# Moving the end of an expert chunk into the next chunk, and reading the expert weights in rows of 2 KB instead of 16 KB

## The reference, cut to what matters

```python
def expert_ffn(xb, wg, wu, wd):
    return (jax.nn.silu(xb @ wg) * (xb @ wu)) @ wd
...
    h2 = rms_norm(x, lp['norm2_g'])
    moe = hier_moe(h2.reshape(B * T, D), ...)      # sum over a token's two experts of gate * expert_ffn(h2)
    x = x + moe.reshape(B, T, D)
...
    y_prompt = rms_norm(yp, final_norm_g)          # and the same for y_sample
```

## Time and profile before

| | |
|---|---|
| time, median of 3 runs | 1856.1 us (1854.3 to 1857.44) |
| the profiled execution's own time | 1861.37 us |
| its span, first to last instruction | 1859.8 us |
| the first half and the router, up to the first chunk's matmuls | 868.6 us |
| 32 chunks, from there to the start of the last one | 944.0 us |
| the last chunk and what comes behind it | 47.2 us |

### The profile page before, as it was taken

How to read it: one execution, slowest core, us unless ns; L and a number is a source line. 1 busy time by engine, 2 the same in 40 slices (tenths; PEclk the granted TensorE clock), 3 DMA queues, 4 the chain that set the end, 5 groups by cost and what they waited for, 6 DMA issues and landing times.

```text
span 1859.8 us, 29119 instructions
## 1 busy us (share of the span) xinstructions
PE 1715.0 (92%) x10574; PEld 1464.1 (79%) x10574; DVE 704.1 (38%) x1890; ACT 371.7 (20%) x799; POOL 491.3 (26%) x872
## 2 busy tenths in 40 slices
PE   7999999999999999975999999999898789698985
PEld 4767676767676767655999999998898789688985
DVE  3446464636363636453232222222223132222232
ACT  2313131313131313121121111110101011101111
POOL 1001010101111111112333333333434243334444
PEclk9999999999999999995999999999999899799997
DMA  9310101010202020255887988888888788767761
GB/s 310 121 69 24 68 23 68 23 68 7 83 0 90 0 79 1 58 142 188 266 298 256 318 300 277 289 281 298 277 297 283 258 278 291 280 239 285 259 207 51
DMA packets 89329, 325.76 MB, mean 175 GB/s; under 512 B 31653, under 2 KB 32582, under 8 KB 81094
## 3 DMA queue, kind: packets, MB, share of 16 engines
q1 hardware_dynamic: 56870, 253.67, 38.5%
q0 software_dynamic: 32416, 71.49, 12.5%
HBM read 283.66 MB, written 65.98 MB: 188 GB/s over the span
## 4 chain that ended last, share of the span: by engine, by line
PE 54%; DMA 23%; issue 9%; POOL 6%; DVE 5%; POOLq 2%; ACT 1%; DVEq 1%; ACTq 0%; SPq 0%
PE ps L703 18%; DMA gate_sb<-acc_rows,idx_out 14%; PE ps L764 13%; PE ps L726 6%; DMA acc_rows<-w_out_sb,idx_out 6%; PE ps L839 6%; PE ps L851 3%; DVE w_out_sb L1326 3%; DMA idx_in<-slot_table 2%; PE ps L785 2%; PE ps L736 1%; POOL acc_rows L655 1%; DVE gate_sb L1333 1%; POOL out_y L671 1%; POOL pad L339 1%
## 5 line engine op out<-in xcount | busy, mean ns | idle before, releaser
L839 PE MATMUL ps<-w_out_sb,w_in_sb 128*128 128x156 f32 (+4 forms) x3072 | 395.8, 286 | 1.3 <-ACT w_out_sb L978 1.3
L839 PEld LDWEIGHTS ps<-w_out_sb,w_in_sb 128*128 128x128 f32 x3072 | 387.5, 190 | 1.6 <-issue 1.6
L339 POOL TENSOR_TENSOR pad<-mhalf 128x1 f32<-128x1 f32 x260 | 57.2, 220 | 1169.3 <-DMA idx_in<-slot_table 272.6
L703 PE MATMUL ps<-cols_sb,w_in_sb 128*128 128x256 f32 (+1 forms) x1728 | 360.5, 369 | 2.7 <-issue 2.7
L703 PEld LDWEIGHTS ps<-cols_sb,w_in_sb 128*128 128x128 f32 x1728 | 313.6, 191 | 45.9 <-issue 6.9
L764 PE MATMUL ps<-w_out_sb,cols_sb 128*128 128x512 f32 x544 | 236.7, 596 | 5.5 <-DVE cols_sb L1156 5.5
L764 PEld LDWEIGHTS ps<-w_out_sb,cols_sb 128*128 128x128 f32 x544 | 103.3, 191 | 132.6 <-issue 126.7
L991 ACT ACTIVATE w_out_sb<-w_out_sb 78x1024 f32<-78x1024 f32 (+4 forms) x64 | 67.6, 1057 | 605.6 <-DVE w_out_sb L1326 604.6
L851 PE MATMUL ps<-w_out_sb,cols_sb 128*128 128x156 f32 (+4 forms) x1024 | 151.5, 317 | 22.2 <-DVE w_out_sb L1316 22.2
L851 PEld LDWEIGHTS ps<-w_out_sb,cols_sb 128*128 128x128 f32 x1024 | 148.5, 218 | 23.6 <-DVE w_out_sb L1316 23.6
L1326 DVE SCALAR_TENSOR_TENSOR w_out_sb<-ps,idx_out,gate_sb 64x512 f32<-64x512 f32 (+4 forms) x128 | 87.0, 738 | 205.8 <-DMA gate_sb<-acc_rows,idx_out 205.8
(11 more groups left out here) (194 smaller groups left out, 1593.0 us busy)
## 6 DMA issues: line engine op xcount, KB each, us to landing
w_in_sb<-in_w_gate SPq DMA_DIRECT2D x32, 2048.0 KB, 8.9
w_in_sb<-in_w_up SPq DMA_DIRECT2D x16, 2048.0 KB, 16.2
w_in_sb<-in_w_down SPq DMA_DIRECT2D x16, 2048.0 KB, 13.5
rows_sb<-in_w_up SPq DMA_DIRECT2D x16, 2048.0 KB, 15.8
cols_sb<-in_w_down SPq DMA_DIRECT2D x16, 2048.0 KB, 12.2
rows_sb<-in_x SPq DMA_DIRECT2D x34, 512.0 KB, 3.7
acc_rows<-rows_sb SPq DMA_DIRECT2D x17, 512.0 KB, 2.6
h_rows<-cols_sb SPq DMA_DIRECT2D x17, 512.0 KB, 2.7
```

Of the source, the lines that this page charges most:

```text
L339: return eng.tensor_tensor(pad[:, n:n + 1], mhalf[:, 0:1], mhalf[:, 0:1], ALU.mult)
L703: mm = pe.matmul(bank[:, cc * n:(cc + 1) * n], w_in_v[:, k, col:col + P], hT[:, k, 0:n], start=(k == 0), stop=(k == KD - 1))
L839: mm = pe.matmul(bank[:, m * CH:m * CH + size], w[:, k, f * P:(f + 1) * P], xTm[:, k, :, 0:size // 2], start=(k == 0), stop=(k == KD - 1))
```

## The change

The parts, of which the sixth concerns the first half:

1. The `r` banks are evicted plainly: ACT copies `r00` and `r10`, DVE `r01` and `r11`, each 512 columns, into `ysb`.
2. Gate and addition become two instructions of DVE from SBUF (`add_rows`), which run in the next chunk, behind its first L1316. The sums of squares (`row_squares`) stand on ACT behind the next chunk's second Silu, the scaling (`norm_rows`) on DVE behind its third L1316.
3. POOL's loop starts with the scatter of the chunk before and its root, waits for that scatter to land, gathers `part` for its own chunk, scatters the finished rows of the chunk before, and then loads `idx_in` and gathers `xg`. Ahead of the loop there is a gather of `part` with a list that names no row, and behind it the root and the output of the last chunk.
4. Gate and up matrices are read as eight rows of 2 KB per partition. (The down matrix was read in rows of 4 KB before and still is.)
5. New semaphores order this: `added`, `none_loaded`.
6. `h2` is written in its natural order, by the same instruction without the strided view, and the router's two small matrices are loaded row by row to match.

```diff
 def gate_up(e, i):
     for dst, src in ((wg_e[i], a["w_gate"]), (wu_e[i], a["w_up"])):
-        sp.dma_start(dst.rearrange("p k f -> p (k f)"), src.rearrange("e (p k) f -> e p (k f)", p=P)[bass.ds(e, 1)]
-                     .rearrange("a p n -> p (a n)")).then_inc(w_loaded[i][0], 16)
+        sp.dma_start(dst, src.rearrange("e (k p) f -> e p k f", p=P)[bass.ds(e, 1)]
+                     .rearrange("a p k f -> p (a k) f")).then_inc(w_loaded[i][0], 16)
...
+load_index_at(NE * SLOTS, idx_out, none_loaded)
...
+def roots(n):
+    pool.wait_ge(y_stored, 32 * n + 32)
+    pool.wait_ge(ysq_ready, 2 * n + 3)
+    carried(6 * n + 2)
+    nc.gpsimd.tensor_copy(idx_y[:], idx_out[:]).then_inc(iy_ready, 1)
...
+pool.wait_ge(none_loaded, 16)
+fetch_rows()
+with pool.Fori(0, chunks) as q:
+    pool.wait_ge(added, 2 * q + 2)
+    carried(6 * q + 1)
...
+    roots(q)
+    pool.wait_ge(nx_loaded, 16 * q + 16)
+    pool.wait_ge(iy_ready, q + 1)
+    pool.wait_ge(part_stored, 32 * q + 32)
+    carried(6 * q + 3)
+    nc.gpsimd.tensor_copy(idx_out[:], idx_nx[:]).then_inc(io_ready, 1)
+    pool.wait_ge(io_ready, q + 1)
+    carried(6 * q + 4)
+    fetch_rows()
+    load_index(q + 1, idx_nx, nx_loaded)
+    store_rows(q, 6 * q + 5)
...
+def row_squares(n):                                  # ACT
+    for h in range(2):
+        act.wait_ge(added, 2 * n + 1 + h)
+        act.wait_ge(ysq_ready, 2 * n + 1 + h)
+        act.wait_ge(yrs_ready, n + 1)
+        nc.scalar.activation(junk, ysb[:, h], ACT.Square, accum_out=ssq[0:HF, h:h + 1]).then_inc(ysq_ready, 1)
...
+    act.wait_ge(part_stored, 32 * q + 32)
+    act.wait_ge(yfin_ready, 2 * q + 2)
+    for i in range(2):
+        bank = wait_full(act, "chunk", q, f"r{i}0")
+        nc.scalar.copy(ysb[0:size // 2, 0, i * BANK:(i + 1) * BANK], bank[0:size // 2, :])\
+            .then_inc(read("chunk", f"r{i}0"), 1)
...
+def add_rows(n):                                     # DVE
+    dve.wait_ge(part_loaded, 32 * n + 32)
+    for h in range(2):
...
+        V.scalar_tensor_tensor(out=ysb[:, h], in0=ysb[:, h], scalar=idx_out[:, h, 1:2].bitcast(F32),
+                               in1=part[:, h], op0=ALU.mult, op1=ALU.add).then_inc(added, 1)
+
+def norm_rows(n):
+    dve.wait_ge(yrs_ready, n + 2)
...
-    V.scalar_tensor_tensor(out=by_k(h2[:, t], 0), in0=by_k(xr[:, t], 1), scalar=rstd[:, GT + t:GT + t + 1],
-                           in1=by_k(g2b[:], 1), op0=ALU.mult, op1=ALU.mult).then_inc(h2_ready[t], 1)
+    V.scalar_tensor_tensor(out=h2[:, t], in0=xr[:, t], scalar=rstd[:, GT + t:GT + t + 1], in1=g2b[:],
+                           op0=ALU.mult, op1=ALU.mult).then_inc(h2_ready[t], 1)
```

More of the change, by code:

```diff
@@ L297, in hymba_step @@
         nx_loaded = sem("nx_loaded")
+        none_loaded = sem("none_loaded")
         io_ready = sem("io_ready")
@@ L300, in hymba_step @@
         part_stored = sem("part_stored")
+        added = sem("added")
         iy_ready = sem("iy_ready")
@@ L390, in _ @@
                 (rb[:], a["router_b"].broadcast_to([P, NG + NE])),
[L391 to L392 removed]
+                (rw[:, :, 0:NG], a["router_gw"].rearrange("(k p) n -> p k n", p=P)),
+                (rw[:, :, NG:NG + NE], a["router_ew"].rearrange("(k p) n -> p k n", p=P)),
             ]
@@ L627, in _, with fetch_rows @@
                 pool.dma_start(idx_y[:, h, :], table[0:CH].rearrange("(p h) c -> p h c", h=2)[:, h, :]).then_inc(y_stored, 16)
+            load_index_at(NE * SLOTS, idx_out, none_loaded)
             pool.nop().then_inc(yrs_ready, 1)
             pool.nop().then_inc(moe_carry, 1)
[L630 to L636, removed]
+            def fetch_rows():
                 for h in range(2):
@@ L646, in _ @@
                 wait_full(pool, "chunk", q, "xT3")
-                carried(5 * q + 3)
+                carried(6 * q + 6)
                 gather()
[L650 to L674, removed]
+            carried(6 * chunks + 1)
+            roots(chunks)
+            pool.wait_ge(iy_ready, chunks + 1)
+            store_rows(chunks, 6 * chunks + 3)
             pool.wait_ge(xg_loaded, 32 * chunks + 64)
             pool.wait_ge(nx_loaded, 16 * chunks + 16)
-            pool.wait_ge(y_stored, 32 * chunks + 32)
+            pool.wait_ge(part_stored, 32 * chunks)
+            pool.wait_ge(y_stored, 32 * chunks + 64)
         @block.tensor
@@ L979, in x_columns @@
                         .then_inc(read(seg, f"xT{j}"), 1)
+            def row_squares(n):
+                for h in range(2):
+                    act.wait_ge(added, 2 * n + 1 + h)
+                    act.wait_ge(ysq_ready, 2 * n + 1 + h)
+                    act.wait_ge(yrs_ready, n + 1)
+                    nc.scalar.activation(junk, ysb[:, h], ACT.Square, accum_out=ssq[0:HF, h:h + 1]).then_inc(ysq_ready, 1)
             def chunk(q, size):
@@ L984, in chunk @@
                     nc.scalar.activation(sg[:, f, 0:size], bank[:, 0:size], ACT.Silu).then_inc(sg_ready, 1)
+                    if f == 1:
+                        row_squares(q)
                 x_columns("chunk", q, size)
[L986 to L992, removed]
+                act.wait_ge(part_stored, 32 * q + 32)
[4 more added lines that the diff above has]
+                        .then_inc(read("chunk", f"r{i}0"), 1)
             act.nop().then_inc(ysq_ready, 1)
@@ L1000, in _ @@
                     chunk(q, size)
+            row_squares(ends[-1])
         @block.vector
@@ L1310, in _ @@
             ends = size_ends(dve)
+            def add_rows(n):
+                dve.wait_ge(part_loaded, 32 * n + 32)
+                for h in range(2):
+                    for i in range(2):
+                        wait(dve, read("chunk", f"r{i}{h}"), JOBS.before("chunk", n, f"xT{2 * i + h}"))
+                    V.scalar_tensor_tensor(out=ysb[:, h], in0=ysb[:, h], scalar=idx_out[:, h, 1:2].bitcast(F32),
+                                           in1=part[:, h], op0=ALU.mult, op1=ALU.add).then_inc(added, 1)
+            def norm_rows(n):
+                dve.wait_ge(yrs_ready, n + 2)
+                dve.wait_ge(y_stored, 32 * n + 32)
+                for h in range(2):
+                    V.scalar_tensor_tensor(out=yfin[:, h], in0=ysb[:, h], scalar=rstd[0:HF, h:h + 1],
+                                           in1=g1b[0:HF], op0=ALU.mult, op1=ALU.mult).then_inc(yfin_ready, 1)
             def chunk(q, size):
@@ L1317, in chunk @@
                         .then_inc(read("chunk", f"gu{f}"), 1)
+                    if f == 0:
+                        add_rows(q)
+                    if f == 2:
+                        norm_rows(q)
                 for j in PAIRS:
@@ L1320, in chunk @@
                     V.tensor_copy(yT[:, 2 * j:2 * j + 2, 0:size], pair(bank, size)).then_inc(read("chunk", f"y{j}"), 1)
-                dve.wait_ge(io_ready, q + 1)
-                dve.wait_ge(part_loaded, 32 * q + 32)
+                dve.wait_ge(part_stored, 32 * q + 32)
+                dve.wait_ge(ysq_ready, 2 * q + 3)
                 for i in range(2):
[L1324 to L1334, removed]
+                    bank = wait_full(dve, "chunk", q, f"r{i}1")
+                    V.tensor_copy(ysb[0:size // 2, 1, i * BANK:(i + 1) * BANK], bank[0:size // 2, :])\
+                        .then_inc(read("chunk", f"r{i}1"), 1)
             dve.wait_ge(fg_loaded, 16)
@@ L1339, in _ @@
                     chunk(q, size)
+            add_rows(ends[-1])
+            norm_rows(ends[-1])
 def kernel(**inputs):
```

15 lines of the change are left out of this document (13 added, 2 removed).

## The result

The changed kernel takes 1803.25 us (median of 4 runs, 1799.3 to 1806.86), the kernel before 1856.77 beside it (1854.3 to 1863.93): a ratio of 0.9705, 95% interval 0.9669 to 0.9741. The forecast was 1804. As the experiments show, that figure hides two effects of opposite sign: the rows of 2 KB alone give more than the whole gain, and the new order takes some 18 us of it back. Two executions (one of the kernel before, one of `pieces_4kb_b`) took far longer than every other of the same kernel, 3,710 and 8,421 us, and are left out of the times and ratios measured here (the 1820 in a later expectation still has the second in it).

The account below looks back on a forecast made before the run. POOL's round was taken to bound the last 19 periods. Short periods 54.5, chunks of 156 4.4 and `h2` 0.8 less, start 8 more: 51.7 us off 1861.4, 1809.7, or 1804 on the runs' scale; forecast 1780 to 1835, whole range 1755 to 1875.

Parts of the forecast that it names:

- POOL's round sets the pace of the short chunks: Last 19 periods, 30.37 us each: POOL's round, not PE, sets them; changed round forecast at 27.5 us.
- The 1.2 us: POOL's round in the kernel before: its terms summed to 29.2 us, within 1.2 of the mean period; half was kept.
- landing with root: POOL's round: root leaves the path, the scatter's whole landing takes its place, 6.1 us a round.
- The short periods: The 19 periods of the last three stretches: from 30.37 to 27.5 us each, 54.5 us less.
- the chunks of 156: Chunks of 156 slots: a round falls below PE's own work, stretch from 234.7 to 230.3 us, 4.4 less.
- The first chunk: Ahead of the loop: empty list and gather, then added steps, delay PE's down matmuls to 900, 8 us once.
- The 0.8 us of `h2`: L1170 without the strided view: 0.8 us shorter 17 times, but counted only behind the last tile, 0.8 us.
- The 2 KB pieces decide: POOL's queue beside gate and up loads: 82 GB/s instead of 51, so 3 us less waiting for `idx_in` a round.
- Without any help from the queue a round is 29.8 us: POOL's round, pieces giving nothing: 14.0 + 6.1 + 9.7 us; as a rival about 1875 us, chance 0.07.
- the slower rival: POOL's wait for `part_stored` ahead of the gather: long landings, pieces no help, round 32.6, 1932 us; chance 0.16.
- PE alone: Short stretches: POOL's round falls below PE's work, 470 us instead of 577, 1752 us in all; chance 0.10.
- The DMA engines as bound: Short periods: DMA work with some idle time leaves 28.5 us, 1823 in all; chance 0.09 with other smaller gains.

Follow-up runs that it names:

- pieces_4kb_b: The changed kernel with gate and up read in 4 KB pieces, two neighbouring rows each, `h2` paired to match: 1813.65 us, ratio 0.9751 to the kernel before.
- rows_only: The kernel before with the 2 KB rows and the matching order of `h2` and router matrices, old eviction and order: 1785.19 us, ratio 0.9614.
- order_only: The changed kernel with gate and up in 16 KB pieces and strided `h2` as before, new round kept: 1952.01 us, ratio 1.0486 to the kernel before.
- start_early: The changed kernel with the empty list loaded at POOL's first lists and its gather issued early: 1794.54 us, ratio 0.9633 to the kernel before.
- rows_strided: The kernel before with only gate and up read as 2 KB rows, `h2` still strided: 1788.78 us, ratio 0.9624.
- rows_list: The kernel before with the 2 KB rows and `idx_in`'s load at the head of POOL's round: 1785.21 us, ratio 0.9576.
- list_start: The changed kernel with `idx_in`'s load ahead of the gather of `part`, and the empty list and its gather early: 1774.75 us, ratio 0.9523 to the kernel before.

## Why the prediction was right, and where it was not

**POOL's round sets the pace of the short chunks: right.** The round's parts, with POOL's waits of the 19 short rounds alone: 14.0 of issuing, 1.4 of root and 4.1 (77.3/19) of landing, 7.4 (141.2/19) of list, 26.9 us; the 19 periods are 27.2 each, forecast 27.5. The 1.2 us that the forecast's sum for the kernel before left open came of waits averaged over the whole second half: in its 19 short rounds the list is 188.3/19 = 9.9 and the scatter 42.4/19 = 2.2, and 14.0 + 4.1 + 9.9 + 2.2 = 30.2 of 30.4. Two terms were off and cancelled, which was luck: landing with root is 5.5 where the forecast had 6.1, the list 7.4 where it had 6.7. The rest of the distance to 27.5 is half of that 1.2.

**Term by term.** The short periods gave 60.7 us (forecast 54.5) and the chunks of 156 gave 7.5 (4.4), because the chunks of 156 had the higher level of the clock, 2.4 GHz, throughout (1.00). The first chunk cost 8.4 (8): POOL waited for the empty list, the gather went out at 884.53, and PE began its down matmuls 6.0 us late:

```profile
884.53 1.07 POOL L636 DMA_INDIRECT gate_sb<-acc_rows,idx_out  x1 [8.39 <-DMA idx_out<-slot_table]
...
898.48 12.03 PE L870 MATMUL ps<-w_out_sb,w_in_sb 128*128 128x180 f32 x64 [7.39 <-DVE w_out_sb L1355]
```

The forecast had 900 for that start, 1.5 more; what makes the 8 come out is that the matmuls themselves then took 12.03 us, where they took 9.96 before, at a mean granted clock of 0.84 instead of 1.00. The forecast had no such term. DVE's extra work, 1.1 us a chunk by the forecast, is 1.4 in the chunks of 132 (54.86 against 46.44 over six), and lies beside other work. The 0.8 us of `h2` can't be told from nothing.

**The 2 KB pieces decide: right, and shown; where they act, only in part.** The step took 82 GB/s for POOL's queue beside them; the stretch above shows 128. In the old order the pieces do what the forecast said: the list falls from 9.9 to 7.2 us a short round (137.7/19 in `rows_only`). In the new order the list hardly falls, from 8.2 in `order_only` (155.7/19) to 7.4, and the landing with root falls from 12.1 (1.4 + 204.0/19) to 5.5. The forecast kept the landing at 6.1 with or without the pieces. Why the list fell by less than the rate of the queue rose is not shown. The Trainium skill (DMA: Bandwidth & Descriptors, "Queues, rings and completion order") gives a typical packet, the unit in which an engine changes queues, as some 9 to 17 descriptors; read as widely as a whole load's share it would have given nothing, and the pieces gave 72 us. Whether the number itself holds here the counts above do not show. The same page's section "SWDGE vs HWDGE vs iDMA" calls a packet that GpSimd writes preferably at most 4096 bytes; the rows of POOL's queue here are 4096 bytes each, and the page says no such thing of SP's pieces.

**"Without any help from the queue a round is 29.8 us: one wait replaces another, and nothing is won": wrong.** `order_only` is that case, and its 19 periods are 34.0 us. The term that failed is the landing. I took 6.1 us from the old order, where most rounds never waited; in the short rounds of the new one it is the 12.1 above. The round becomes 14.0 + 12.1 + 8.2 = 34.3. That is the slower rival, which I had at 32.6 and 1932 us and to which I gave 0.16: its place was right and its price near, its condition (no help from the pieces) did not hold for the changed kernel, and the load that its scatter meets is gate and up, not the down matrix. I had not seen that a late round of POOL puts the scatter beside that load in most short rounds.

**So the total was right, but the credit was not.** I gave the order a start cost and 0.6 us a round and the pieces 3. Measured, the pieces alone take 72 us off (1856.8 to 1785.2); the order then adds 18: 8.7 at the start (`start_early`) and 8.5 in the short periods (516.3 less 507.8). The intervals of the two ratios just touch (0.9672 is the upper end of the one, 0.9669 the lower end of the other), but `rows_strided` and `rows_list`, in the old order too, took 1789 and 1785 us. Its landing and longer list (4.0 + 7.0, against 1.4 + 6.1 in `rows_only`) outweigh the 2.7 us of scaling that left the path. Asked of the two halves, the forecast missed both: 1790 to 1815 us for the rows alone, measured 1785, and 1855 to 1885 for the order alone, measured 1952.

**The other rivals.** *PE alone* (470 us for the short stretches) was not reached; `list_start` comes to 496.4, its first short stretch on PE alone. *The DMA engines as bound*: their share is 0.92 in the changed kernel and 0.97 to 0.99 in the chunks of 140 and 132 of `list_start`, so they may be next; no run took load off them, and what holds the last 5 to 10 us of its chunks of 132 and 128 stays open.

## What to carry to other kernels

Where two queues share the DMA engines, the length of one queue's pieces can set the waits of the other, as it did here: before moving waits about in program order, look at what a small load waits beside, and shorten those pieces. A step that is moved may come to stand beside a large load: here the scatter of `order_only` met 4 MB of weights in half of its rounds. Test the parts of a compound change apart even when the total comes out as forecast: here one part was worth 72 us and the other cost 18, until two small edits (the list ahead of the gather, an earlier start) made the new order the faster by 10 us (1774.75 against 1785.21 with the same early list, with intervals that overlap a little).

## What was not expected of the hardware

Beside one row of POOL's queue went about two of SP's pieces, whether they held 16 KB or 4 (1.7 and 2.1), so that POOL's share of the engines' time was 13% beside 16 KB and 48% beside 1 KB. And shorter pieces had a price mostly in company: alone, 2 KB and 16 KB pieces moved nearly the same, but beside POOL's queue both together moved 2.19 MB in 6 us at 16 KB, 1.94 at 4 KB, 1.85 at 2 KB and 1.68 at 1 KB. Other stretches gave 2.00 to 2.48 at 16 KB, 1.73 to 1.92 at 4, 1.76 to 1.83 at 2 and 1.74 to 1.80 at 1, so the fall behind 16 KB stands and the order of the other three does not.
